# Two transformer blocks in one launch: the gated linear attention's levels two to a PE visit, and the masked copies ahead of a low half

## What is computed

```python
# per chunk of 64 tokens; state0 = 0; b = cumulative sum of log_a in the chunk
diff  = bcum[:, :, :, None, :] - bcum[:, :, None, :, :]
decay = exp(where(causal, diff, -inf))
attn  = einsum('bhtk,bhsk,bhtsk->bhts', qt, kt, decay)
o     = einsum('bhtk,bhkv->bhtv', qt * exp(bcum), state) + attn @ vt
state = exp(blast)[..., None] * state + einsum('bhsk,bhsv->bhkv', kt * exp(blast - bcum), vt)
```

## Time and profile before

| | |
|---|---|
| median of 3 runs | 805.94 us (805.93 to 806.11) |
| profiled execution | 805.84 us, span of the core 804.0 us |
| granted TensorE clock | 1.000 of full speed over the span |
| busy share: PE, DVE, ACT, POOL | 99%, 74%, 59%, 5% |
| the chain that ended last | PE 96%, DVE 2%, DMA 1% |
| the loop over t | from about 351 to 488 us of the span |

### The profile page before, as it was taken

One profiled execution on the slowest core, in us unless ns is written; L12 is line 12 of the kernel. 1 busy time (PEld: TensorE's weight loads), 2 busy tenths in 40 slices (PEclk: granted clock), 3 DMA queues, 4 the chain that ended last, 5 costly groups with the idle time before them and its releaser, 6 DMA issues.

```text
span 804.0 us, 12564 instructions
## 1 busy us (share of the span) xinstructions
PE 799.2 (99%) x4860; PEld 690.4 (86%) x4860; DVE 591.2 (74%) x920; ACT 472.5 (59%) x692; POOL 42.6 (5%) x88
## 2 busy tenths in 40 slices
PE   9999999999999999999999999999999999999998
PEld 8878889888888888888888889999998888888886
DVE  6897789987878888677988863686576755566654
ACT  6876456655665666867566555655844744444442
POOL 0000000000000000003242510100000000000000
PEclk9999999999999999999999999999999999999999
DMA  9943344664665563654454463334365656655551
GB/s 329 357 166 106 106 157 158 209 210 159 207 205 174 195 234 135 240 168 158 172 183 159 156 208 107 105 107 147 125 201 161 182 182 209 208 175 191 172 193 53
DMA packets 90351, 142.08 MB, mean 177 GB/s; under 512 B 3840, under 2 KB 56768, under 8 KB 90176
## 3 DMA queue, kind: packets, MB, share of 16 engines
q1 hardware_dynamic: 89728, 140.38, 52.4%
q10 hardware_dynamic: 576, 1.05, 0.4%
HBM read 140.37 MB, written 1.05 MB: 176 GB/s over the span
## 4 chain that ended last, share of the span: by engine, by line
PE 96%; DVE 2%; DMA 1%; SPq 1%; issue 0%
PE bank L511 22%; PE bank L512 21%; PE bank L513 21%; PE bank L600 14%; PE bank L605 8%; PE bank L382 3%; PE bank L1121 1%; PE bank L1144 1%; DMA vec<-in_vectors 1%; PE bank L1057 1%; PE bank L584 1%; DVE w_lo L1779 1%; SPq L413 0%; PE bank L587 0%; PE bank L742 0%; PE bank L1081 0%
## 5 line engine op out<-in xcount | busy, mean ns | idle before, releaser
L1779 DVE TENSOR_TENSOR w_lo<-raw,w_hi 128x1024 fp32r<-128x1024 f32 (+1 forms) x254 | 302.0, 1214 | 59.2 <-ACT w_hi L1271 58.6
L1271 ACT CAST w_hi<-raw 128x1024 fp32r<-128x1024 f32 (+1 forms) x254 | 260.1, 1045 | 114.4 <-PE bank L513 111.6
L511 PE MATMUL bank<-w_hi,h_both 128*128 128x512 f32 (+1 forms) x336 | 133.5, 397 | 0.1
L512 PE MATMUL bank<-w_lo,h_both 128*128 128x512 f32 (+1 forms) x336 | 130.4, 388 | 0.0
L513 PE MATMUL bank<-w_hi,h_both 128*128 128x512 f32 (+1 forms) x336 | 130.4, 388 | 0.0
L600 PE MATMUL bank<-a_both,w_hi 128*128 128x512 f32 x512 | 121.5, 389 | 0.0
L600 PEld LDWEIGHTS bank<-a_both,w_hi 128*128 128x128 f32 x512 | 95.5, 188 | 19.4
L511 PE MATMUL bank<-w_hi,a_both 128*128 128x512 f32 (+1 forms) x270 | 106.4, 394 | 0.0
L512 PE MATMUL bank<-w_lo,a_both 128*128 128x512 f32 (+1 forms) x270 | 104.9, 388 | 0.0
L513 PE MATMUL bank<-w_hi,a_both 128*128 128x512 f32 (+1 forms) x270 | 104.8, 388 | 0.0
L511 PEld LDWEIGHTS bank<-w_hi,h_both 128*128 128x128 f32 x336 | 63.3, 188 | 14.8 <-issue 2.4
(11 more groups left out here) (235 smaller groups left out, 1057.2 us busy)
## 6 DMA issues: line engine op xcount, KB each, us to landing
raw<-in_w_in SPq DMA_DIRECT2D x45, 1024.0 KB, 5.1
raw<-in_w_up SPq DMA_DIRECT2D x22, 1024.0 KB, 5.0
raw<-in_w_ff_up SPq DMA_DIRECT2D x16, 1024.0 KB, 5.4
raw<-in_w_ff_down SPq DMA_DIRECT2D x16, 1024.0 KB, 4.8
raw<-in_w_down SPq DMA_DIRECT2D x11, 1024.0 KB, 4.9
raw<-in_w_out SPq DMA_DIRECT2D x8, 1024.0 KB, 5.0
raw<-in_w_gla_branch SPq DMA_DIRECT2D x4, 1024.0 KB, 5.0
raw<-in_w_attn_branch SPq DMA_DIRECT2D x2, 1024.0 KB, 5.0
```

Source lines behind the costliest of these rows:

```text
L511: nc.tensor.matmul(dst, l_hi, r_hi, start=start, stop=False)
L512: nc.tensor.matmul(dst, l_hi, r_lo, start=False, stop=False)
L1271: nc.scalar.copy(dst, raw_half(m % RAW, half, size, cols)).then_inc(s.hi_done, 1)
L1779: nc.vector.tensor_tensor(dst, raw_half(n // 2 % RAW, n % 2, size, cols), h, ALU.subtract).then_inc(s.lo_done, 1)
```

## The change

Five things are changed in the code.

1. A table LEVEL_VISITS says which levels PE does at the end of which chunk and into which bank: levels 8 and 0 behind chunk 1, 2 and 1 behind chunk 3, 4 and 3 behind chunk 5, 6 and 5 behind chunk 7, and 7 behind chunk 8. The first level of a pair goes into banks 6 and 7, those of the head transposes, the second into banks 4 and 5.
2. The head transposes wait until the level in banks 6 and 7 has been copied out; a visit waits until ACT has taken the transposes.
3. DVE's copies of a visit stand between low halves 3 and 4 instead of at the end of the step; the second of a pair waits for the first (gla_taken).
4. qe and ke have two buffers in turn. The second ones lie in the columns of r_row, which moves, and of dil.
5. So dil is loaded behind the last level but for the slabs: SP waits for nine levels before dil and the last two slabs of the loop.

```diff
+LEVEL_VISITS = {1: ((LEVELS + 1, 6), (0, 4)), 3: ((2, 6), (1, 4)), 5: ((4, 6), (3, 4)), 7: ((6, 6), (5, 4)), 8: ((7, 4),)}
+TAKEN_BEFORE = {t: sum(len(v) for at, v in LEVEL_VISITS.items() if at < t) for t in range(12)}
...
-        r_row = area(2048, TOKENS)
+        r_row = area(12160, TOKENS)
...
+        level_qk = ((qe, ke), (area(2048, GH, TOKENS), area(24864, GH, TOKENS)))
...
-            sp.wait_ge(s.x_added, 1)
+            for m in range(M_IN2 + 5, M_R + 2):
+                load(m)
+            sp.wait_ge(s.gla_level, LEVELS + 2)
             sp.dma_start(dil, consts[:, C_DIL:C_LEVEL].rearrange("p (a c) -> p a c", a=TT)).then_inc(s.dil_in, 16)
-            for m in range(M_IN2 + 5, M_FF2):
+            for m in range(M_R + 2, M_FF2):
                 load(m)
...
+                pe.wait_ge(s.gla_taken, TAKEN_BEFORE[t + 2] - (len(LEVEL_VISITS.get(t + 1, ())) == 2))
                 turn_tiles(4, lambda a, k: a_tok[:, t % 3, a, k * P:(k + 1) * P], s.att_turned, (6, 7))
...
-            def level(t):
-                q_, k_ = (gqT, gkT) if t == 8 else (qe, ke)
-                pe.wait_ge(s.gla_qe, min(t + 1, 8))
-                if t == 0:
-                    pe.wait_ge(s.row_taken, 1)
-                else:
-                    pe.wait_ge(s.gla_taken, t)
+            def level(t, first):
+                q_, k_ = (gqT, gkT) if t == LEVELS + 1 else level_qk[t % 2]
+                if t <= LEVELS:
+                    pe.wait_ge(s.gla_qe, t + 1)
...
-                if 1 <= t <= 9:
-                    level(t - 1)
+                for nth, (lv, first) in enumerate(LEVEL_VISITS.get(t, ())):
+                    if nth == 0:
+                        pe.wait_ge(s.row_taken, 1)
+                        if t > 1:
+                            pe.wait_ge(s.gla_taken, TAKEN_BEFORE[t])
+                    if first == 6 and t > 1:
+                        pe.wait_ge(s.att_T, 2 * ((t - 2) // 3) + min((t - 2) % 3 + 1, 2))
+                    level(lv, first)
...
-                    nc.vector.tensor_tensor(flat(qe), flat(gqT), z, ALU.mult)
-                    nc.vector.tensor_tensor(flat(ke), flat(gkT), z, ALU.mult).then_inc(s.gla_qe, 1)
+                    q_, k_ = level_qk[(t - 1) % 2]
+                    nc.vector.tensor_tensor(flat(q_), flat(gqT), z, ALU.mult)
+                    nc.vector.tensor_tensor(flat(k_), flat(gkT), z, ALU.mult).then_inc(s.gla_qe, 1)
...
-                lo(n + 6, n + 7)
+                lo(n + 6)
+                for nth, (lv, first) in enumerate(LEVEL_VISITS.get(t, ())):
+                    dve.wait_ge(s.gla_level, TAKEN_BEFORE[t] + nth + 1)
+                    if nth > 0:
+                        dve.wait_ge(s.gla_taken, TAKEN_BEFORE[t] + nth)
...
+                lo(n + 7)
...
-                if 1 <= t <= 9:
-                    dve.wait_ge(s.gla_level, t)
-                if t == 1:
-                    nc.vector.tensor_copy(flat(g_cross), bank[:, 4, :]).then_inc(s.gla_taken, 1)
```

More of the change, by code:

```diff
@@ L1031, in turn_heads @@
                     pe.wait_ge(s.att_T, nth)
+                pe.wait_ge(s.gla_taken, TAKEN_BEFORE[t + 2] - (len(LEVEL_VISITS.get(t + 1, ())) == 2))
                 turn_tiles(4, lambda a, k: a_tok[:, t % 3, a, k * P:(k + 1) * P], s.att_turned, (6, 7))
-            def level(t):
-                q_, k_ = (gqT, gkT) if t == 8 else (qe, ke)
-                pe.wait_ge(s.gla_qe, min(t + 1, 8))
-                if t == 0:
-                    pe.wait_ge(s.row_taken, 1)
-                else:
-                    pe.wait_ge(s.gla_taken, t)
+            def level(t, first):
+                q_, k_ = (gqT, gkT) if t == LEVELS + 1 else level_qk[t % 2]
+                if t <= LEVELS:
+                    pe.wait_ge(s.gla_qe, t + 1)
                 for hd in range(GH):
                     if t == 0:
-                        ins = nc.tensor.matmul(bank[:, 4, hd * P:(hd + 1) * P], k_[:, hd, 0:P], q_[:, hd, P:2 * P],
+                        ins = nc.tensor.matmul(bank[:, first, hd * P:(hd + 1) * P], k_[:, hd, 0:P], q_[:, hd, P:2 * P],
                                                start=True, stop=True)
@@ L1050, in level @@
                             if t == 1:
-                                ins = nc.tensor.matmul(bank[0:half, 4 + hd // 2, at + half:at + P],
+                                ins = nc.tensor.matmul(bank[0:half, first + hd // 2, at + half:at + P],
                                                        k_[:, hd, a * P:a * P + half], q_[:, hd, a * P + half:(a + 1) * P],
@@ L1056, in level @@
                                 c = a * P + e * half
-                                ins = nc.tensor.matmul(bank[e * half:(e + 1) * half, 4 + hd // 2,
+                                ins = nc.tensor.matmul(bank[e * half:(e + 1) * half, first + hd // 2,
                                                             at + e * half:at + (e + 1) * half],
@@ L2268, in _ @@
                     level_distance(t)
-                lo(n + 6, n + 7)
+                lo(n + 6)
[3 more added lines that the diff above has]
+                        dve.wait_ge(s.gla_taken, TAKEN_BEFORE[t] + nth)
+                    if lv == 0:
+                        nc.vector.tensor_copy(flat(g_cross), bank[:, first, :]).then_inc(s.gla_taken, 1)
+                        continue
+                    at = LEVELS if lv > LEVELS else LEVELS - lv
+                    mask = levels[:, at:at + 1, :].bitcast(I32).to_broadcast([P, 8, P])
+                    nc.vector.copy_predicated(g_in.rearrange("p h a t -> p (h a) t"), mask,
+                                              bank[:, first:first + 2, :].rearrange("p b (n t) -> p (b n) t", t=P)).then_inc(
+                                                  s.gla_taken, 1)
+                lo(n + 7)
                 heads = t < 3 * AG and t % 3 < 2
```

## The result

The changed kernel takes **808.19 us** (median of 9 runs, 808.10 to 808.37) where the kernel before, on the same chip, takes 805.94 (805.81 to 806.11): a ratio of 1.0027, 95% interval 1.0018 to 1.0035. It is 2.25 us slower; the forecast was 1.9 slower, 807.8. The profiled execution has a span of 806.4 us, where that of before had 804.0, at the same granted TensorE clock of 1.000.

A forecast was written before the change was run, and what follows sets the result against it. PE, busy 99% of the span, was taken as the bound, with DVE second just ahead of it. A saving of 1.03 us and stalls of 0.6, 1.0 and 1.3 sum to +1.9: 807.8 us, range 806.8 to 811.6.

The forecast's parts named there:

- What PE saves: PE's level visits: three joined pairs each shed one edge of 0.345 us, saving 1.03 us in all.
- Rival 4: PE's joined visits save nothing; stalls shrink by as much, total stays +1.9 us; chance 0.62 together with the forecast.
- What DVE loses: DVE's new order: guess later by the copies, no copy covers POOL; 7.26 us from last guess step to L2252.
- the walk: DVE's lateness followed through iterations 1 to 8, giving PE stalls of 0.6, 1.0 and 1.3 us.
- Rival 1: POOL shut out until DVE pauses (4.57 us step, 8.15 us chain): +5.5 us, 811.4 us; chance 0.26.
- Rival 2: DVE not late at all, PE keeps its 1.03 us saving: 804.9 us; chance 0.09.
- chunk 3, third quarter (low half): PE wants this low half at 393.54, DVE now ends it at 394.1: stall 0.6 us.
- chunk 6, transposes (banks 6 and 7): PE's head transposes wait for the copy out of banks 6 and 7, ending at 433.26: stall 1.0 us.
- chunk 9, transposes (count of copies): PE's transposes wait for all nine copies, level 7's ending at 472.62: stall 1.3 us.
- The rest of the change: Second qe and ke buffers, moved r_row, the visit's wait for ACT, late dil and two held slabs: no cost.
- rival 3: The two held slabs land late, each further us costing PE one; 808.8 us with one; chance 0.03.

The follow-up runs named there:

- the kernel with split copies: Changed kernel with the narrow wait, copies of levels 8, 4, 3 and 6 ahead of the fourth low half, the others behind the guess: 804.98 us.
- the narrow count: Changed kernel, but the head transposes wait only for copies that used banks 6 and 7, not for level 7's: 806.78 us.

## Why the prediction was right

**What PE saves** was 1.05 us for 1.03. A pair costs what was worked out from one visit's weight loads, 2.205; level 8 in front of level 0 gives back nothing, as taken (2.175 for 2.18). So an edge of 0.345 is paid once for each run of small levels. Rival 4 (no saving) is refuted by the pair, and by the kernel with split copies, whose gain is that saving. One price behind the 2.205 does not hold as it was put, 0.058 us per place. Level 1 has 8 places where the others have 16, and its visit costs as much, 387.50 - 385.77 = 1.73 us from start to start, as that of level 2 (PE's timeline of the kernel before):

```profile
385.77 0.39 PE L513 MATMUL bank<-w_hi,a_both 128*128 128x512 f32 x1
386.09 1.15 PE L1051 MATMUL bank<-arena 128*64 128x64 f32 x16
...
387.50 0.39 PE L512 MATMUL bank<-w_lo,a_both 128*128 128x512 f32 x1
```

Level 1 stands on both sides of the sum, so the saving is untouched. Why 8 places cost as much as 16 is open.

**What DVE loses** went by the walk. From guess to over_rms it is 7.25 or 7.26 us in every chain but the first (7.29), by the reason given: with the guess directly ahead of the product, POOL's first step meets the product and takes 1.1. Rival 1 (8.15, 811.4 us) is refuted: no POOL step above 1.2 us. Rival 2 (no stall) is refuted by the waits of 2.5 us ahead of L2265.

**The stalls** came at the three places named and at no other, each a little larger than forecast:

| | forecast | measured, from starts |
|---|---|---|
| chunk 3, third quarter (low half) | 0.6 | 0.80 |
| chunk 6, transposes (banks 6 and 7) | 1.0 | 1.13 |
| chunk 9, transposes (count of copies) | 1.3 | 1.38 |
| saved by visits | -1.03 | -1.05 |
| sum | +1.9 | +2.3 |

The term that was mis-sized is the walk of DVE. It took a pair of copies as 2.63 us, and from the first copy's start to the next instruction it is 459.28 - 456.59 = 2.69 in step 7 (2.68 in step 5, 2.73 in step 3), as the second copy starts some 0.10 behind the first one's end; over_rms of iteration 8 comes at 469.33, where 465.35 + 3.56 and the 0.17 of this execution's later start of DVE's loop give 469.08. And it took nothing for the way from a copy's end to PE's start, which is 0.15 at chunk 9. Both were in the range given ("a signal or two of 0.1 us", "the copy pair at 2.52 or 2.75"); the prediction names no row for the 0.1 of a signal, and what the runs show for it are these 0.10 and 0.15.

One part of the reasoning was too short. The stall at chunk 9 was put down to the transposes waiting for all nine copies, which is so; but the prediction did not ask whether they must. They use banks 6 and 7, level 7 stands in 4 and 5, and the narrow count gives back the whole of it.

**The rest of the change** cost nothing, as forecast. The late slabs made ACT wait 5.13 us and PE not at all, so rival 3 did not come; the kernel with that part alone shows it by 0.0 us. The second buffers of qe and ke were not run alone; the kernel with split copies has them too and keeps the whole saving.

## What to carry to other kernels

A joined visit saves its edge (0.345 us three times here) only if nothing on PE has to wait for what the join moved; list, for each buffer that gets a second use, the instant at which its next user wants it, and wait for that user's own count and no other. An engine with idle time can still be on the path: a later guess, and 14.4 us instead of 12.6 of DVE's waiting for short POOL steps, were enough to bring a copy's end behind PE's need, though the same order cost nothing where no transposes waited for a copy. Where work is moved ahead of something urgent, move only what is itself waited for: three of the nine copies were (a fourth went along, in a step without a guess), and putting the others back, with the narrow wait, turned +2.25 us into -1.04.

## What the runs showed of the hardware

A short POOL instruction (0.20 to 0.23 us alone) takes 1.05 to 1.25 us beside a product or a low half on DVE (128x1024, both inputs in SBUF), until that one is over. Beside a masked copy out of PSUM it takes 0.20 to 0.23, as if alone; this one lies beside the copy of 404.44 (POOL's timeline of the kernel before):

```profile
405.50 0.22 POOL L503 TENSOR_TENSOR heads_newton<-heads_newton 128x16 f32<-128x16 f32 x1
```

But a step that runs across the end of such a masked copy with a product behind it, or begins at most 0.02 us behind that end, takes 4.57 to 4.73 us, until the two products and two low halves behind the copy are over and DVE pauses; 19 such steps were seen, and none behind a plain copy out of PSUM or behind the guess. The cause is open. The Trainium skill (SBUF — State Buffer, "SBUF: two separate sides") says that whichever starts first, a GpSimd instruction or a DVE instruction of certain kinds (one with two inputs in SBUF is among them), holds the shared port pair for the whole instruction. The steps of 1.1 us agree; the long ones do not, since DVE started three or four further instructions while POOL's stood waiting.
